# Rows of the paged cache gathered by four tokens and transposed on VectorE in 32x32 blocks, in place of TensorE transposes

## The chip, the cores and the metric

One core of one Trainium2 chip. The metric is the device time of one execution in microseconds. A core has TensorE (PE, with its weight loads PEld), VectorE (DVE), ScalarE (ACT), GpSimd (POOL) and SyncE (SP); each runs its own queue of instructions in order and waits for others by semaphores. SyncE and GpSimd also issue the transfers (DMA) spoken of here.

## What is computed

One step of a decoder layer: a norm, one wide input projection, sparse attention with three branches, a gated MLP branch, an output projection and a final norm, for 512 prompt tokens and for 8 sequences of 4 new tokens with 1,024 cached tokens each. All is in fp32. The change touches only the compression of keys and values, cut here to what matters:

```
CMP_BLOCK, CMP_STRIDE, CMP_HIDDEN, PAGE_SIZE = 32, 16, 128, 128
def compress(rows, params):                       # rows: (B, T, 2 heads, 64)
    w1, b1, w2, b2 = params                       # w1: (32 * 64, 128), w2: (128, 64)
    n_cmp = (T - CMP_BLOCK) // CMP_STRIDE + 1
    idx = arange(n_cmp)[:, None] * CMP_STRIDE + arange(CMP_BLOCK)[None, :]
    blocks = rows[:, idx].transpose(0, 1, 3, 2, 4).reshape(B, n_cmp, G, CMP_BLOCK * dh)
    return gelu(blocks @ w1 + b1) @ w2 + b2
kc = compress(concatenate([pool_k[page_table], k_cmp]), cmp_k)   # sequences: 63 blocks each
vc = compress(concatenate([pool_v[page_table], v_cmp]), cmp_v)
kc, vc of the prompt: compress(k_cmp), compress(v_cmp)           # 31 blocks
```

Each block is 32 tokens by 64 channels of one head, multiplied by w1, a sum over 2,048 values. On the chip it is 16 matmuls that each sum over 128 partitions, so the cached rows, which lie in memory as token by channel, have to be turned so that channels lie on partitions.

## The kernel before

A function `plan()` writes one list of steps, `ORDER`. Every engine walks the same list and does its part of each step, so the list sets the order within each queue, and semaphores set the rest. The steps `main` are groups of 24 fp32r matmuls of the big projections (each fp32 operand is split in a high and a low part, and three products are summed; L1735). The rest of the work is placed between them.

The compression has ten chunks. Chunk 0 is the prompt's keys, 1 to 4 two sequences each for the keys, 5 the prompt's values, 6 to 9 two sequences each for the values (`PAIRS` are the eight cached chunks). The steps of a cached chunk `c`:

- GpSimd (`load`, L912) gathers 128 rows of 8 tokens, 4 KB each, of one sequence into one of three slots of `ring` by an indirect DMA, 512 KB in all; two gathers a chunk. It waits until TensorE has transposed what the slot held.
- `xt` n (n = 0 to 3): TensorE transposes half a slot by four 128x128 transposes (L1881) into one of two PSUM banks `t`, which other steps use too. ScalarE casts it to fp32r as the high part `xt_hi` in two instructions of 64 partitions (L1152). VectorE subtracts to get the low part `xt_lo`, again in halves of 64 partitions (L1456), and does one of ScalarE's casts (L1449). In the list, `xt` 2 and 3 cut the main group of the chunk into three parts (`part`).
- `hidh`: 32 matmuls, w1's high and low parts by `xt_hi` (L1917, L1918). `hidl`: 16 matmuls, w1's high part by `xt_lo` (L1920); it is placed behind the first transposes of the next chunk. ScalarE applies the gelu.
- `kc`: small matmuls with w2 (L1933, L1938), and VectorE adds the bias and for keys the rotation.

A prompt chunk has one `xt` with eight small transposes (L1885), four copies on VectorE (L1439), and one set of 16 plain fp32 matmuls `hid` (L1896).

Also in the stage: `low` and `split` of the next weights (VectorE L1301, ScalarE L1034), which release the next weight loads on SyncE; the layer norm steps `ln`, `ln2` (VectorE); the spatial gate `sp` (TensorE L1871, VectorE L1383 to L1393); `w1hi` and `w1lo`, the split of w1 for keys and later for values. SyncE ties 16 small copies of the query blocks to the step (`xt`, 2, 0) and window-cache copies to `xt` of chunks 1, 3, 6 and 8. GpSimd ties its gathers and, at (`xt`, 9, 0), the first key loads to these steps. `hidh` and `kc` wait also for gelu results, and `xt` of a chunk may overwrite `xt_hi` after `hidh` of the chunk before and `xt_lo` after its `hidl`.

## Time and profile before

| | us |
|---|---|
| three runs, median | 566.74 (565.77 to 567.42) |
| profiled execution, span from first to last instruction | 562.9 |
| the compression stage in it | about 98 to 225 |

The profiled execution has no time of its own on record beside its span; the median lies 3.8 us above the span. In the profile PE and PEld are TensorE's matmuls and weight loads, DVE is VectorE, ACT ScalarE, POOL GpSimd and SP SyncE. L1735 is line 1735 of the kernel before. `t` are the two PSUM banks of the transposes, `so` the PSUM banks of the compression and the scores, `m` those of the main groups, `U` one large SBUF area that holds, among others, the ring. TensorE overlaps successive matmuls, so the distance from one start to the next is what one of them holds, and it is less than its listed duration. "Idle before" is the time that an engine had nothing to do just before an instruction, with what ended it.

### The profile page before, as it was taken

The page shows a single profiled execution, that of the slowest core. Times are in us where ns is not written, and L with a number is a line of the kernel's source. Part 1 is how long each engine was busy: PE and PEld are TensorE (multiplying, and loading weights), DVE is VectorE, ACT ScalarE, POOL GpSimd, SP SyncE. Part 2 cuts the span into 40 slices and gives each one's busy share as a digit, 9 for nine tenths or more (in the row PEclk, how much of TensorE's full clock was granted, in tenths as well). Part 3 has the DMA queues.
Part 4 walks back from the last instruction along what each step waited for, and adds up shares of the span by engine and source line. Part 5 has one row for each costly group of instructions (what it writes and reads, how often), then busy time and mean ns, then how long its engine had stood idle before and what let it go on. Part 6 is the DMA issues. An engine that isn't in the chain of part 4 may idle for free.

```text
span 562.9 us, 12929 instructions
## 1 busy us (share of the span) xinstructions
PE 540.9 (96%) x5214; PEld 490.3 (87%) x5214; DVE 344.9 (61%) x854; ACT 257.2 (46%) x585; POOL 135.0 (24%) x237
## 2 busy tenths in 40 slices
PE   6899999999999999999999999999999999999995
PEld 4899999999988899898897877767788999999995
DVE  5633231398797778567465488686864367773466
ACT  5533424554713443324133378677775352223343
POOL 0016423121201141372400035656336000000000
PEclk9999999999999999999999999999999999999999
DMA  8537822537335452586831155656445624305104
GB/s 296 194 98 230 266 76 77 187 113 216 104 112 208 134 169 76 167 283 243 273 104 40 38 138 149 178 129 157 117 114 133 172 76 146 126 30 186 42 4 158
DMA packets 60239, 81.06 MB, mean 144 GB/s; under 512 B 7506, under 2 KB 48914, under 8 KB 59923
## 3 DMA queue, kind: packets, MB, share of 16 engines
q1 hardware_dynamic: 49088, 49.97, 29.1%
q0 software_dynamic: 10368, 29.14, 16.8%
q10 hardware_dynamic: 722, 1.12, 0.5%
q8 instruction: 42, 0.69, 0.5%
q14 instruction: 19, 0.15, 0.1%
HBM read 65.23 MB, written 8.13 MB: 130 GB/s over the span
## 4 chain that ended last, share of the span: by engine, by line
PE 67%; DVE 7%; issue 1%; ACT 1%; DVEq 0%; ACTq 0%
PE m L1735 44%; PE so L2043 4%; PE so L2050 3%; PE so L1917 2%; PE so L1918 2%; PE so L1920 2%; PE t L1881 2%; PE so L1956 1%; PE so L2004 1%; DVE w_lo L1301 1%; DVE xt_sb L1456 1%; PE m L1819 1%; PE so L2030 1%; PE t L2023 1%; PE t L1979 1%
## 5 line engine op out<-in xcount | busy, mean ns | idle before, releaser
L1735 PE MATMUL m<-h_hi,w_hi 128*128 128x272 f32 x448 | 133.9, 299 | 0.8 <-DVE za L1414 0.5
L1735 PE MATMUL m<-h_hi,w_lo 128*128 128x272 f32 x448 | 129.2, 288 | 0.0
L1735 PE MATMUL m<-h_lo,w_hi 128*128 128x272 f32 x448 | 128.8, 287 | 0.0
L1735 PE MATMUL m<-w_hi,h_hi 128*128 128x256 f32 (+2 forms) x360 | 104.3, 290 | 2.4 <-issue 1.9
L1735 PE MATMUL m<-w_hi,h_lo 128*128 128x256 f32 (+2 forms) x360 | 101.8, 283 | 0.0
L1735 PE MATMUL m<-w_lo,h_hi 128*128 128x256 f32 (+2 forms) x360 | 101.8, 283 | 0.0
L1301 DVE TENSOR_TENSOR w_lo<-raw,w_hi 128x1024 fp32r<-128x1024 f32 (+2 forms) x62 | 71.0, 1154 | 42.9 <-ACT w_hi L1034 42.8
L1735 PEld LDWEIGHTS m<-h_hi,w_hi 128*128 128x128 f32 x448 | 84.3, 188 | 12.2 <-issue 9.6
L1735 PEld LDWEIGHTS m<-h_lo,w_hi 128*128 128x128 f32 x448 | 84.5, 189 | 0.0
L1735 PEld LDWEIGHTS m<-h_hi,w_lo 128*128 128x128 f32 x448 | 84.4, 188 | 0.0
L990 POOL DMA_DIRECT2D U<-p_turn x108 | 58.3, 548 | 102.4 <-DVE p_turn L1641 101.3
L1735 PEld LDWEIGHTS m<-w_hi,h_hi 128*128 128x128 f32 (+1 forms) x360 | 67.7, 188 | 3.9 <-issue 2.1
L1735 PEld LDWEIGHTS m<-w_lo,h_hi 128*128 128x128 f32 (+1 forms) x360 | 68.0, 189 | 0.1
L1735 PEld LDWEIGHTS m<-w_hi,h_lo 128*128 128x128 f32 (+1 forms) x360 | 67.7, 188 | 0.1
L1034 ACT CAST w_hi<-raw 128x1024 fp32r<-128x1024 f32 (+2 forms) x62 | 60.9, 989 | 0.6 <-DMA raw<-in_w_in 0.5
L1456 DVE TENSOR_TENSOR xt_sb<-t,xt_sb 64x512 fp32r<-64x512 f32 x64 | 44.1, 689 | 9.9 <-PE so L1920 5.2
L1152 ACT CAST xt_sb<-t 64x512 fp32r<-64x512 f32 x56 | 32.5, 580 | 37.7 <-PE t L1881 36.4
L1617 DVE CUSTOM_DVE_ANT_0 U<-so,cst 128x512 f32<-128x512 f32 (+3 forms) x64 | 28.7, 484 | 20.1 <-PE so L2043 20.0
L1209 ACT ACTIVATE U<-U,st 128x512 f32<-128x512 f32 (+3 forms) x64 | 30.7, 551 | 18.3 <-DVE st L1630 18.3
L1735 PE MATMUL m<-x_hi,w_lo 128*128 128x272 f32 x128 | 36.8, 288 | 0.0
L1735 PE MATMUL m<-x_hi,w_hi 128*128 128x272 f32 x128 | 36.8, 287 | 0.0
L1735 PE MATMUL m<-x_lo,w_hi 128*128 128x272 f32 x128 | 36.8, 287 | 0.0
(306 smaller groups left out, 935.3 us busy)
## 6 DMA issues: line engine op xcount, KB each, us to landing
raw<-in_w_in SPq DMA_DIRECT2D x36, 512.0 KB, 4.5
U<-in_x_p SPq DMA_DIRECT2D x8, 512.0 KB, 5.5
raw<-in_w_o SPq DMA_DIRECT2D x8, 512.0 KB, 3.5
U<-p_turn POOLq DMA_DIRECT2D x54, 64.0 KB, 2.6
U<-p_turn SPq DMA_DIRECT2D x42, 64.0 KB, 2.9
raw<-in_w_in SPq DMA_DIRECT2D x8, 256.0 KB, 3.9
raw<-in_w_pa SPq DMA_DIRECT2D x8, 256.0 KB, 4.0
...
```

The costliest lines, as they stand in the source:

```text
L990: pool.dma_start(*block_move(s[1], n)).then_inc(p_moved_pool[s[1] % 4], 16)
L1034: ins = nc.scalar.copy(hi, x)
L1152: ins = nc.scalar.copy(turned(xt_hi, r, g, b), TB[t % 2][64 * g:64 * g + 64, :].rearrange("p (q o n) -> p q o n", q=4, o=2))
L1209: ins = nc.scalar.activation(pb[u][:, j, 0:n], pb[u][:, j, 0:n], ACT.Copy, scale=st[:, m + 12 + j:m + 13 + j])
L1301: ins = v.tensor_tensor(lo, x, hi.bitcast(F32), ALU.subtract)
L1456: ins = v.tensor_tensor(turned(xt_lo, r, g, b), TB[(t + m - n) % 2][64 * g:64 * g + 64, :].rearrange("p (q o n) -> p q o n", q=4, o=2), tu ...
L1617: v.tensor_tensor_reduce(pb[u][:, a, 0:n], S[k % 3][:, 0:n], cs("causal")[:, 512 - n:512], 1.0, -3e38, ALU.add, ALU.max, st[:, m + a:m + a ...
L1735: ins = mm(out, lhs(a, k), rhs(b, k), start=(k == 0 and a + b == 0), stop=(k == n - 1 and a == 1))
L1881: ins = pe.transpose(tb[:, q * P:(q + 1) * P], x[:, (2 * q + r) * P:(2 * q + r + 1) * P], ident)
L1917: mm(out[:, 0:256], w, xt_hi[:, x], start=(j == 0), stop=False, skip_group_check=True)
L2043: mm(S[k % 3][:, 0:n], qT[r, 2 * jh + jj, tok(i)], kT[r, y, 0:n], start=True, stop=True).then_inc(p_scored, 1)
L2050: ins = mm(O[64 * g:64 * g + 64, 256 * jh:256 * jh + 256].rearrange("p (j a r) -> p j a r", j=2, a=4), v_tok[:, y, k, g * DH:(g + 1) * DH] ...
```

## The change

The cached rows are gathered by 4 tokens (2 KB) rather than 8, with 128 rows or 256 KB to a gather, four to a chunk; a ring slot holds one such piece and half of the old ring's space becomes three buffers `xt_f`. VectorE turns a whole piece with one transpose of 128x512 in 32x32 blocks from the slot into `xt_f`; partition 32 a + i then holds channel i of a block for the tokens of quarter a, and the rows of w1 are permuted in memory to agree (`quarters`), which also makes its load one 8 KB run per partition. New steps `xh` (ScalarE casts a piece, 128 partitions at a time) and `xl` (VectorE subtracts it) take the place of the halves. The prompt chunks do the same with one piece each, which `hid` reads directly from `xt_f`. The main group is no longer cut by transposes. The transposes `xt` are put in the list one chunk ahead for three pieces and within the chunk for the fourth. The slot is freed by VectorE's transpose (`x_turned`) and `xt_f` by `xl` (`xt_lo_done`) or `hid`.

```diff
-CMP_ROW = 2 * (np.arange(P) % 64) + np.arange(P) // 64
+CMP_GROUP = np.arange(P) % 32
...
     put("group_mod", (p % 16)[:, None])
-    put("cmp_mod", (CMP_ROW % 16)[:, None])
+    put("cmp_mod", (CMP_GROUP % 8 * 4 + p // 32)[:, None])
     return c
...
              7: [("sp", 4), ("mix", u0[0]), ("mix", u0[1])], 8: [("mix", u1[0]), ("mix", u1[1])], 9: [("mix", u1[2])]}
-    order += [("w1hi", 0), ("xt", 0, 0)]
+    turns = iter([("xt", c, n) for c in range(NCH) for n in range(4 if c in PAIRS else 1)])
+    def turn(count):
+        order.extend(itertools.islice(turns, count))
+    order += [("w1hi", 0)]
+    turn(3)
     main(3)
     order += [("hid", 0), ("w1lo", 0)]
+    turn(1)
     for c in range(1, NCH):
...
         if c == 5:
-            order += [("xt", 5, 0)] + behind + [("sp", 0), ("w1hi", 1), ("ln2", 1), ("w1lo", 1), ("ln2", 2), ("ln2", 3), ("hid", 5),
-                                                ("kc", 4), ("sp", 1)]
+            order += behind + [("sp", 0), ("w1hi", 1), ("ln2", 1), ("w1lo", 1), ("ln2", 2), ("ln2", 3), ("hid", 5), ("kc", 4), ("sp", 1)]
+            turn(1)
             main(1)
             continue
-        order += [("xt", c, 0), ("xt", c, 1)] + behind
+        order += [("xh", c, n) for n in range(3)] + behind + [("xl", c, 0)]
+        turn(1)
+        order += [("xh", c, 3)]
         if c == 1:
...
         s, after = take()
-        order += [("part", s, 0, 5), ("xt", c, 2), ("part", s, 5, 7), ("xt", c, 3), ("part", s, 7, 8), ("kc", c - 1), ("hidh", c)]
+        order += [("part", s, 0, KD)] + [("xl", c, n) for n in range(1, 4)] + [("kc", c - 1), ("hidh", c)]
+        turn(3)
         order += ([s] if c != 7 else []) + [x for x in after if x not in (("ln", NT), ("lnr",))] + extra.get(c, [])
...
 RING = 3
-LOADS = [(w, b) for w in ("kc", "vc") for b in ["p"] + list(range(NB))]
-LOAD_AT = {x: n for n, x in enumerate(LOADS)}
+TURNS = [s for s in ORDER if s[0] == "xt"]
+TURN_AT = {s[1:]: n for n, s in enumerate(TURNS)}
 NKEY = 3 * QB
...
-def load_of(c, n):
-    return LOAD_AT[("kc" if c < 5 else "vc", "p" if c % 5 == 0 else 2 * (c % 5 - 1) + n // 2)]
-def load_turned(n):
-    w, b = LOADS[n]
-    c = 0 if w == "kc" else 5
-    return T_AT[("xt", c, 0) if b == "p" else ("xt", c + 1 + b // 2, 2 * (b % 2) + 1)] + 1
 def ring_count(n):
-    return sum(32 if LOADS[k][1] == "p" else 16 for k in range(n % RING, n + 1, RING))
+    return sum(16 if TURNS[k][1] in PAIRS else 64 for k in range(n % RING, n + 1, RING))
...
-        ring = U[:, 8200:11272].rearrange("p (r c) -> p r c", r=RING)
+        ring = U[:, 8200:9736].rearrange("p (r c) -> p r c", r=RING)
+        xt_f = U[:, 9736:11272].rearrange("p (r c) -> p r c", r=RING)
         w1_at = [U[:, 11272:13320].rearrange("p (j n) -> p j n", j=16), za[:, :, :].rearrange("p j t -> p (j t)")[:, 0:2048].rearrange("p (j n) -> p j n", j=16)]
...
         xt_hi, xt_lo = xt_sb[:, 0:2050], xt_sb[:, 2050:4100]
-        xtp = [x[:, 0:512].rearrange("p (q g m) -> p q g m", q=4, g=G) for x in (sg_flat, U)]
         hid_at = [U[:, 13320:13576], U[:, 13576:13832]]
...
-        def turned(x, r, g, b):
-            return x[64 * r:64 * r + 64, 0:2048].rearrange("p (q o g b n) -> p q o g b n", q=4, o=2, g=G, b=2)[:, :, :, g, b, :]
+        def turned(x, c, n):
+            b, half = divmod(n, 2)
+            return x[:, 0:2048].rearrange("p (k b m i) -> p k b m i", b=2, m=2, i=32)[:, :, b, half, :]
+        def in_blocks(c, n):
+            return xt_f[:, TURN_AT[c, n] % RING, :].rearrange("p (k i) -> p k i", i=32)
...
                 elif s[0] == "load_w1":
-                    sp.dma_start(w1_at[0], w1k.rearrange("(j p) n -> p j n", p=P)).then_inc(w1_loaded[0], 16)
-                    sp.dma_start(w1_at[1], w1v.rearrange("(j p) n -> p j n", p=P)).then_inc(w1_loaded[1], 16)
+                    sp.dma_start(w1_at[0], w1k).then_inc(w1_loaded[0], 16)
+                    sp.dma_start(w1_at[1], w1v).then_inc(w1_loaded[1], 16)
                 elif s[0] == "xt" and s[2] == 0 and s[1] % 5 in (1, 3):
...
-            def load(n):
-                w, b = LOADS[n]
-                if n >= RING:
-                    pool.wait_ge(t_done, load_turned(n - RING))
-                dst, done = ring[:, n % RING, :], ring_loaded[n % RING]
-                if b == "p":
+            def load(t):
+                _, c, n = TURNS[t]
+                if t >= RING:
+                    pool.wait_ge(x_turned, t - RING + 1)
+                dst, done = ring[:, t % RING, :], ring_loaded[t % RING]
+                if c not in PAIRS:
                     pool.wait_ge(cmp_out, 32)
-                    src = (pk_cmp if w == "kc" else pv_cmp).rearrange("(m o r) c -> o m (r c)", o=2, r=8)
-                    for o in range(2):
+                    src = (pv_cmp if c else pk_cmp).rearrange("(m o r) c -> o m (r c)", o=4, r=4)
+                    for o in range(4):
                         pool.dma_start(dst[32 * o:32 * o + 32, :], src[o, :, :]).then_inc(done, 16)
                 else:
-                    src = {"kc": ck_cmp, "vc": cv_cmp}[w]
-                    pool.indirect_dma_start(dst, None, src, bass.IndirectOffsetOnAxis(cmp_rows[:, b:b + 1], 0)).then_inc(done, 16)
+                    b = 2 * (c % 5 - 1) + n // 2
+                    src = ck_cmp if c < 5 else cv_cmp
+                    pool.indirect_dma_start(dst, None, src, bass.IndirectOffsetOnAxis(cmp_rows[:, n % 2, b:b + 1], 0)).then_inc(done, 16)
...
                     pool.dma_start(s_chunk, vg[0:TS, NT, :]).then_inc(out_done, 16)
-                elif s[0] == "xt" and s[2] % 2 == 0:
-                    load_upto(load_of(s[1], s[2]) + RING + 1)
+                elif s[0] == "xt":
+                    load_upto(TURN_AT[s[1:]] + RING + 1)
                     if s[1:] == (NCH - 1, 0):
...
                     ins.then_inc(w1_hi_done, 1)
-                elif kind == "xt" and s[1] in PAIRS:
-                    c, n = s[1], s[2]
-                    b, r = divmod(n, 2)
-                    act.wait_ge(t_done, t + 1)
+                elif kind == "xh":
+                    _, c, n = s
+                    act.wait_ge(x_turned, TURN_AT[c, n] + 1)
                     if c > 1:
                         act.wait_ge(hid_half, PAIRS.index(c))
-                    if c == 6:
-                        act.wait_ge(hid_sum, 6)
-                    for g in range(G - n // 3):
-                        ins = nc.scalar.copy(turned(xt_hi, r, g, b), TB[t % 2][64 * g:64 * g + 64, :].rearrange("p (q o n) -> p q o n", q=4, o=2))
-                    ins.then_inc(xt_hi_done, 1)
+                    nc.scalar.copy(turned(xt_hi, c, n), in_blocks(c, n)).then_inc(xt_hi_done, 1)
                 elif kind in ("hid", "hidl"):
...
                 elif kind == "xt":
-                    c, n = s[1], s[2]
-                    b, r = divmod(n, 2)
-                    tb = TB[t % 2]
-                    dve.wait_ge(t_done, t + 1)
-                    if c % 5 == 0:
-                        if c:
-                            dve.wait_ge(hid_half, 4)
-                        for r in range(2):
-                            for g in range(G):
-                                ins = v.tensor_copy(xtp[c // 5][64 * r:64 * r + 64, :, g, :],
-                                                    tb[64 * g:64 * g + 64, 256 * r:256 * r + 256].rearrange("p (q m) -> p q m", q=4))
-                        ins.then_inc(t_dve, 1)
-                        continue
-                    if n == 2:
-                        continue
+                    k = TURN_AT[s[1:]]
+                    dve.wait_ge(ring_loaded[k % RING], ring_count(k))
+                    if k >= RING:
+                        c = TURNS[k - RING][1]
+                        if c in PAIRS:
+                            dve.wait_ge(xt_lo_done, 4 * PAIRS.index(c) + TURNS[k - RING][2] + 1)
+                        else:
+                            dve.wait_ge(hid_sum, c + 1)
+                    v.transpose(xt_f[:, k % RING, :], ring[:, k % RING, :]).then_inc(x_turned, 1)
+                elif kind == "xl":
+                    _, c, n = s
+                    dve.wait_ge(xt_hi_done, 4 * PAIRS.index(c) + n + 1)
                     if c > 1:
                         dve.wait_ge(hid_sum, c - (c == 6))
-                    at = PAIRS.index(c)
-                    if n == 3:
-                        v.tensor_copy(turned(xt_hi, 1, 1, 1), tb[64:128, :].rearrange("p (q o n) -> p q o n", q=4, o=2)).then_inc(xt_hi_dve, 1)
-                    for m in range(2 if n == 3 else n, n + 1):
-                        b, r = divmod(m, 2)
-                        dve.wait_ge(xt_hi_done, 4 * at + m + 1)
-                        for g in range(G):
-                            if m == 3 and g == 1:
-                                dve.wait_ge(xt_hi_dve, at + 1)
-                            ins = v.tensor_tensor(turned(xt_lo, r, g, b), TB[(t + m - n) % 2][64 * g:64 * g + 64, :].rearrange("p (q o n) -> p q o n", q=4, o=2),
-                                                  turned(xt_hi, r, g, b).bitcast(F32), ALU.subtract)
-                        ins.then_inc(t_dve, 1)
+                    v.tensor_tensor(turned(xt_lo, c, n), in_blocks(c, n), turned(xt_hi, c, n).bitcast(F32), ALU.subtract).then_inc(xt_lo_done, 1)
                 elif kind == "kc":
...
                     ins.then_inc(t_done, 1)
-                elif kind == "xt":
-                    c, n = s[1], s[2]
-                    ld = load_of(c, n)
-                    pe.wait_ge(ring_loaded[ld % RING], ring_count(ld))
-                    x = ring[:, ld % RING, :]
-                    if c % 5:
-                        r = n % 2
-                        for q in range(4):
-                            ins = pe.transpose(tb[:, q * P:(q + 1) * P], x[:, (2 * q + r) * P:(2 * q + r + 1) * P], ident)
-                    else:
-                        for k in range(8):
-                            r, q = divmod(k, 4)
-                            ins = pe.transpose(tb[:, k * 64:k * 64 + 64], x[0:64, (2 * q + r) * P:(2 * q + r + 1) * P], ident[0:64, 0:64])
-                    ins.then_inc(t_done, 1)
                 elif kind == "hid":
                     c = s[1]
+                    k = TURN_AT[c, 0]
                     pe.wait_ge(w1_loaded[c // 5], 16)
-                    wait_evacuated(pe, T_AT[("xt", c, 0)])
+                    pe.wait_ge(x_turned, k + 1)
                     if c >= 2:
                         pe.wait_ge(hid_ready, c - 1)
+                    x = xt_f[:, k % RING, :].rearrange("p (r g e m) -> p r e g m", r=4, g=G, e=2)
                     for j in range(16):
-                        o = j // 4
-                        at = 32 * (o % 2) + o // 2
-                        ins = mm(S[c % 2][:, 0:2 * NCP], w1_at[c // 5][:, j, :], xtp[c // 5][:, j % 4, :, at:at + NCP], start=(j == 0), stop=(j == 15))
+                        o, r, e = j // 8, j // 2 % 4, j % 2
+                        ins = mm(S[c % 2][:, 0:2 * NCP], w1_at[c // 5][:, j, :], x[:, r, e, :, o:o + NCP], start=(j == 0), stop=(j == 15))
                     ins.then_inc(hid_sum, 1)
...
                         pe.wait_ge(xt_hi_done, 4 * PAIRS.index(c) + 4)
-                        pe.wait_ge(xt_hi_dve, PAIRS.index(c) + 1)
                         if c >= 2:
...
                     else:
-                        for n in range(4):
-                            wait_evacuated(pe, T_AT[("xt", c, n)])
+                        pe.wait_ge(xt_lo_done, 4 * PAIRS.index(c) + 4)
                     for j in range(16):
-                        o, q = divmod(j, 4)
-                        x = slice(512 * q + 256 * (o % 2) + o // 2, 512 * q + 256 * (o % 2) + 256 + o // 2)
+                        o, r, e = j // 8, j // 2 % 4, j % 2
+                        def x(part):
+                            return part[:, 512 * r + o:512 * r + o + 512].rearrange("p (g e n) -> p e g n", g=G, e=2)[:, e, :, :]
                         w = w1_hi[j // 8][:, j % 8, :]
                         if first:
-                            mm(out[:, 0:256], w, xt_hi[:, x], start=(j == 0), stop=False, skip_group_check=True)
-                            ins = mm(out[:, 0:256], w1_lo[:, j, :], xt_hi[:, x], start=False, stop=False, skip_group_check=True)
+                            mm(out[:, 0:256], w, x(xt_hi), start=(j == 0), stop=False, skip_group_check=True)
+                            ins = mm(out[:, 0:256], w1_lo[:, j, :], x(xt_hi), start=False, stop=False, skip_group_check=True)
                         else:
-                            ins = mm(out[:, 0:256], w, xt_lo[:, x], start=False, stop=(j == 15), skip_group_check=True)
+                            ins = mm(out[:, 0:256], w, x(xt_lo), start=False, stop=(j == 15), skip_group_check=True)
                     ins.then_inc(hid_half if first else hid_sum, 1)
...
+    def quarters(a):
+        return A(a).reshape(2, 4, 8, 32, P).transpose(1, 3, 0, 2, 4).reshape(P, 16, P)
     def column(a):
...
         ("x_p", A(x_prompt).reshape(TP, D)), ("x_s", A(x_sample).reshape(TS, D)),
-        ("ck_cmp", A(cache_k_cmp).reshape(-1, 8 * P)), ("cv_cmp", A(cache_v_cmp).reshape(-1, 8 * P)),
+        ("ck_cmp", A(cache_k_cmp).reshape(-1, 4 * P)), ("cv_cmp", A(cache_v_cmp).reshape(-1, 4 * P)),
         ("ck_sel", A(cache_k_sel).reshape(-1, 8 * P)), ("cv_sel", A(cache_v_sel).reshape(-1, 8 * P)),
         ("ck_win", A(cache_k_win).reshape(NB, 512, P)), ("cv_win", A(cache_v_win).reshape(NB, 512, P)),
-        ("pages", np.concatenate([A(page_table).T[np.arange(P) // 16], A(page_table).T[CMP_ROW // 16]], 1)),
-        ("w_in", A(w_in)[0]), ("w1k", A(cmp_k_w1)[0]), ("w1v", A(cmp_v_w1)[0]), ("w_sp", A(w_spatial)[0].transpose(1, 0, 2)),
+        ("pages", np.concatenate([A(page_table).T[np.arange(P) // 16], *(A(page_table).T[4 * m + CMP_GROUP // 8] for m in range(2))], 1)),
+        ("w_in", A(w_in)[0]), ("w1k", quarters(cmp_k_w1)), ("w1v", quarters(cmp_v_w1)), ("w_sp", A(w_spatial)[0].transpose(1, 0, 2)),
         ("w_pa", A(w_pa)[0]), ("w_pb", A(w_pb)[0]), ("w_o", A(w_o)[0]), ("norm_g", A(norm_g).reshape(1, D)), ("final_g", rows(final_g)),
...
```

## Rows read from the trace of the kernel before

**Rows 1.** The page of the kernel before: span and busy time of each engine.
```profile
span 562.9 us, 12929 instructions
...
PE 540.9 (96%) x5214; PEld 490.3 (87%) x5214; DVE 344.9 (61%) x854; ACT 257.2 (46%) x585; POOL 135.0 (24%) x237
```

**Rows 2.** Windows: stretch, its us, busy us (instructions) of PE, PEld, DVE, ACT, POOL, clock, DMA share, GB/s.
```profile
98.00:225.00 127.00, 121.79 (x1079) 116.00 (x1079) 95.07 (x184) 56.09 (x100) 23.82 (x26) 1.00 0.45 146
130.00:142.00 12.00, 11.90 (x104) 11.28 (x105) 9.91 (x21) 5.43 (x11) 2.24 (x3) 1.00 0.65 208
154.00:178.40 24.40, 21.86 (x181) 20.25 (x181) 22.69 (x43) 8.32 (x14) 2.79 (x4) 1.00 0.36 112
```

**Rows 3.** Chain that ended last, one chunk: start us, us, engine, tile, line, count.
```profile
130.91 0.36 PE so L1917
...
134.94 0.88 PE t L1881 x8
...
135.81 1.90 PE so L1920 x16
...
139.59 0.44 PE t L1881 x4
...
142.38 0.36 PE so L1917
```

**Rows 4.** Groups by form, 98 to 225 us: the work the change removes.
```profile
L1881 PE MATMUL t<-cst,U 128*128 128x128 f32 x128 | 19.1, 278 | 2.1 <-DVE sg L1393 2.0
...
L1456 DVE TENSOR_TENSOR xt_sb<-t,xt_sb 64x512 fp32r<-64x512 f32 x64 | 44.1, 689 | 9.9 <-PE so L1920 5.2 <-ACT xt_sb L1152 3.5
...
L1449 DVE CAST xt_sb<-t 64x512 fp32r<-64x512 f32 x8 | 5.6, 695 | 5.7 <-PE t L1881 5.6
...
L1152 ACT CAST xt_sb<-t 64x512 fp32r<-64x512 f32 x56 | 32.5, 580 | 37.7 <-PE t L1881 36.4
```

**Rows 5.** Timeline of PE: transposes of a prompt chunk.
```profile
157.84 0.71 PE L1885 MATMUL t<-cst,U 64*128 64x64 f32 x8
```

**Rows 6.** Groups by form, whole span: nearest rows for what it adds.
```profile
L1494 DVE STREAM_TRANSPOSE U<-U 128x512 f32<-128x512 f32 x19 | 11.9, 673 | 0.0
...
L1301 DVE TENSOR_TENSOR w_lo<-raw,w_hi 128x512 fp32r<-128x512 f32 x8 | 5.1, 678 | 0.0
...
L1034 ACT CAST w_hi<-raw 128x512 fp32r<-128x512 f32 x8 | 4.5, 616 | 0.0
```

**Rows 7.** Chain that ended last: matmuls whose moving operand comes in short runs.
```profile
345.50 1.88 PE so L2050 x16
```

**Rows 8.** DMA issues, 98 to 225 us and then 177 to 183 us: count, median us to landing.
```profile
U<-in_cv_cmp,cmp_rows POOLq DMA_INDIRECT x8, 4.7
...
U<-in_ck_sel,half_rows POOLq DMA_INDIRECT x4, 3.9
...
U<-in_cv_cmp,cmp_rows POOLq DMA_INDIRECT x1, 9.0
```

**Rows 9.** Timelines of DVE and POOL: descriptor writing beside VectorE work.
```profile
124.38 1.21 DVE L1301 TENSOR_TENSOR w_lo<-raw,w_hi 128x1024 fp32r<-128x1024 f32 x1
...
124.63 1.78 POOL L912 DMA_INDIRECT U<-in_ck_cmp,cmp_rows  x1 [5.24 <-PE t L1881]
...
221.87 3.07 DVE L1494 STREAM_TRANSPOSE U<-U 128x512 f32<-128x512 f32 x5
...
223.57 0.95 POOL L931 DMA_INDIRECT turned_late<-in_ck_sel,half_rows  x1 [15.46 <-PE so L1920]
```

**Rows 10.** Timeline of PE: first hi product of chunks 1, 4, 6 and 9.
```profile
119.45 0.35 PE L1917 MATMUL so<-xt_sb,w_hi 128*128 128x256 f32 x1 [0.92 <-DVE xt_sb L1449]
...
153.88 0.36 PE L1917 MATMUL so<-xt_sb,w_hi 128*128 128x256 f32 x1
...
178.39 0.36 PE L1917 MATMUL so<-xt_sb,w_hi 128*128 128x256 f32 x1 [0.36 <-DVE xt_sb L1449]
...
217.35 0.35 PE L1917 MATMUL so<-xt_sb,w_hi 128*128 128x256 f32 x1
```

18 lines of the change are left out of this document (10 added, 8 removed).

## The prediction

> **What bounds the kernel now.** I read the page first, then the busy time by stretch, then the chain of waits through the compression, then the groups of the instructions that the diff touches. The page shows TensorE busy for 540.9 of 562.9 us and no other engine near it [rows 1]. The compression runs from about 98 to 225 us. There TensorE is busy 121.8 of 127.0 us at the full granted clock (1.00, the 2.4 GHz level), VectorE 95.1, ScalarE 56.1 and GpSimd 23.8 [rows 2]. So at most 5.2 us of idle TensorE can be won there; the rest must come from instructions taken off TensorE. Two kinds of stretch differ. In an ordinary chunk (130 to 142 us) TensorE is busy 11.90 of 12.0 us and VectorE 9.91: TensorE sets the pace. In the change from keys to values (154 to 178.4 us) VectorE is busy 22.69 of 24.4 us and TensorE 21.86: there VectorE sets it, with the layer norm, the split of the second w1 and the spatial gate in one queue [rows 2]. The chain of waits through an ordinary chunk is TensorE end to end, from one `hidh` (L1917) at 130.91 to the next at 142.38, 11.47 us. Its transposes stand in that chain as 8 in 0.88 us and twice 4 in 0.44, so 0.11 us for each [rows 3].
>
> **What the change removes.** TensorE: 16 transposes in each of eight cached chunks, 128 in all [rows 4]. Their mean of 278 ns is latency; they follow one another every 0.11 us, so they hold TensorE for 128 x 0.11 = 14.1 us. The two prompt chunks lose 8 half-size transposes each, 8 in about 0.65 to 0.71 us [rows 5], 1.3 us together. That is 15.4 us off the engine that sets the end. With them go the waits for a free `t` bank: the transposes waited 2.1 us, 2.0 of it behind the spatial gate's additions on VectorE (L1393) [rows 4]. One of these waits lies in the VectorE-bound stretch, so I count 1.0. VectorE loses, per cached chunk, 8 subtractions of 689 ns and one copy of 695 ns, 6.2 us; ScalarE loses 7 casts of 580 ns, 4.1 us [rows 4].
>
> **What it adds.** Per cached chunk VectorE gets four 128x512 block transposes and four 128x512 subtractions with both inputs in SBUF, ScalarE four 128x512 casts out of SBUF. All three have near relatives in the trace: the transposes of the keys take 673 ns, the 128x512 weight subtraction 678, the 128x512 weight cast 616 [rows 6]. VectorE: 4 x (0.673 + 0.678) = 5.4 us against 6.2, so 0.8 less; ScalarE 2.5 against 4.1. The old instructions used 64 partitions at a time and the new ones 128, which is why an added job does not add time. Only the prompt chunks and the transition change more: four copies per prompt give way to one transpose. The bounds for these prices are narrow (the strided 32-element runs of the output might cost up to the 695 ns of the slowest row, 0.1 us per chunk).
>
> The matmuls keep their number. Their moving operand changes from one run of 256 columns to two of 128. Matmuls of 256 columns in runs of 32 pace at 1.88/16 = 0.118 us [rows 7], the same as the old `hidl` at 1.90/16 [rows 3]; I take nothing. If each of the 384 matmuls lost 10 ns, it would be 3.8 us; that upper end is my estimate from the resolution of these rows.
>
> GpSimd gets 32 gathers of 256 KB for 16 of 512 KB. It has 100 us of idle time in the stage, and one issue takes about 1 us. What matters is the latency: the old gathers landed in 4.7 us (median), a 256 KB gather of the keys, also in 2 KB rows, in 3.9, and one old gather that met the window-cache copies in 9.0 [rows 8]. The ring still has three slots, but each holds half a batch, so half as much is prefetched, and the slot is freed on VectorE. The third transpose for a chunk uses a slot freed by the fourth of the chunk before. Behind it VectorE has three subtractions, the `kc` step (perhaps 1 of the 3.7 us that its 9.9 holds beside the 6.2 of `xt`) and two transposes, 2.0 + 1.0 + 1.3 = 4.3 us, about the landing time plus the wake-up. The fourth uses the slot freed by the first: until it is wanted TensorE runs `hidh` and `hidl`, 4.0 + 1.9 = 5.9 us [rows 3], so it lands in time unless delayed. Then subtraction, transpose and cast (2.0 us) lie beside the main group and `kc`, 3.8 us (11.5 - 4.0 - 1.9 - 1.8 of transposes): 1.8 us of slack, less what VectorE is late. An undisturbed gather costs nothing, one of 6 us makes VectorE wait but hardly TensorE. Behind a waiting transpose stand the weight split, layer norm and the next subtractions on VectorE, and TensorE's `hidh` waits for them. The 9.0 us gather comes again, where eight window copies go out together near chunk 7: 4.3 us late less the slack and work it covers, about 2 us. I take 2.3 us over the whole stage (0 if nothing is late, about 9 if every chunk loses 1.1).
>
> A contention is to be weighed here. One gather's descriptor writing took 1.78 us, begun while a VectorE subtraction from two SBUF inputs ran, where one beside five block transposes took 0.95 [rows 9]. Taken as a cost, 0.8 us on some gathers fits into the 2.3. The Trainium skill ("SBUF — State Buffer", section "Who interferes with whom") says that `tensor_tensor` with two SBUF inputs takes only the shared read interface, and infers that descriptor writing is not held up; by it this part is zero, by the row up to 0.8 us for a gather, and the trace's single long one speaks mildly against the inference.
>
> The moved steps also carry SyncE work. The 16 copies of the query blocks (`xt` 2,0) and the window copies (`xt` 1, 3, 6, 8) now stand ahead of the weight loads which the same chunk's `low` releases. These weight tiles are split only chunks later, so they cost nothing; without this cover a raw load would be late by the issue time of the 16 copies. The w1 loads become 8 KB runs; they are done long before 98 us, no gain. Key loads on GpSimd follow the last gathers as before.
>
> **The sum.** Chunk 1 waited 0.92 us for its `xt` copies [rows 10]; with the transpose of its fourth piece done about 1 us before TensorE arrives, that goes. Between chunks 4 and 6 (153.88 to 178.39, 24.5 us) VectorE rules, so I followed its queue: it loses 8 subtractions, a copy and 4 prompt copies, about 7.9 us, and gains 5 transposes and about 2 subtractions, 4.7; 3.2 less, of which 0.8 goes back to a wait for the first spatial-gate product. That leaves 2.4, just what TensorE loses there (16 x 0.11 + 0.65), so the stretch keeps its full share and TensorE waits there about as long as now. From chunk 6 to 9 (178.39 to 217.35) three more chunks and 1.0 of bank waits. Total: 15.4 + 0.9 + 1.0 = 17.3, less 2.3 for late gathers, 15.0. After 225 us nothing is changed and TensorE is the bound, so an earlier start is kept. The profiled execution spans 562.9 us, which becomes 547.9. The runs' median, 566.74, lies 3.8 above the span (that execution has no time of its own beside it), and I keep the 3.8: 551.7 us.
>
> **Rivals.**
> Late gathers. The half-size ring makes VectorE wait about 1 to 1.5 us per chunk and the layer norm and splits push it onto TensorE. For it: half the prefetch, the 9.0 us row, two transposes per chunk with no margin. Against: 1.8 us of slack. It gives back a further 4 to 9 us: 556 to 561. Chance 0.18.
> VectorE becomes the bound. In a chunk with layer norm and split it has about 8.7 us (9.9 busy in 12 us scaled to 11.5, less 0.8) of TensorE's 9.7 (11.47 less 1.76). A price 0.15 us higher for each of the eight instructions brings it to 9.9, and with the waits for `hidl` near 10.5: 0.8 us lost on eight chunks, 6.4: 558. Chance 0.07. The Trainium skill ("VectorE: DVE Perf Modes", section "Rules for kernel authors") speaks against the move: a 128x128 transpose belongs on TensorE if PSUM will do, VectorE being the fastest only for 32x32 blocks. The trace agrees on price (0.44 us for four blocks on TensorE, 0.673 on VectorE), but not on what is scarce here.
> Slower. One mechanism: the three-slot ring becomes a round trip. Four pieces per chunk through three slots need 4/3 x (landing + 0.8) us; that passes the old 11.5 us when gathers land in 7.8 us or more. At 9.0 for all, a chunk takes 13.1 us, 1.6 more on six or seven chunks, less the 3 us won outside them: about 574 us. Against: only one gather in the stage took so long. Chance 0.05.
> The change does not pay, because the transposes are hidden anyway: the chain of waits has them in it, so only if VectorE governs every chunk; 565 to 567. Chance 0.03.
> The forecast's own case, 548 to 555: 0.67.
>
> The range reaches from 547.0 (no late gather, most of the remaining idle gone: 566.74 - 19.7) to 560.0, which leaves 0.05 to 0.1 above with the last two rivals and little below. A difference under 0.3% (1.7 us) could not be told from none. Faster 0.91, same 0.03, slower 0.06.
>
> **What would show it.** Right: no PE rows for L1881 and L1885; `hidh` to `hidh` near 9.7 us in chunks 2 to 4; VectorE's transposes near 0.67, subtractions near 0.68, casts near 0.62; TensorE idle for 2 to 3 us ahead of chunk 6 and in chunk 7; 225 us becoming about 210. Wrong: `hidh` matmuls above 0.12 us apiece, transposes ended by a DMA in most chunks, gathers landing in 6 us, or the 15 us won at 225 us given back before the first `qkS`.

## The result, and the profile after

The changed kernel takes 551.43 us (median of 4 runs, 550.79 to 552.57) where the kernel before takes 566.73 (565.77 to 567.42) on the same chip. The ratio on record is 0.9745, 95% interval 0.9724 to 0.9767; the two medians alone give 0.9730, inside it. The profiled execution took 550.91 us itself, with a span of 549.2. That is 13.7 us less span than before, where the medians differ by 15.3.

The page: span, and busy time of each engine (for [rows 1]).

```profile
span 549.2 us, 12605 instructions
...
PE 526.3 (96%) x5070; PEld 478.4 (87%) x5070; DVE 332.7 (61%) x840; ACT 242.0 (44%) x561; POOL 156.4 (28%) x257
```

Windows, columns as in [rows 2]: first the whole stage, then three places that matter below.

```profile
98.00:225.00 127.00, 120.59 (x1148) 115.78 (x1152) 91.59 (x185) 46.60 (x86) 49.23 (x49) 0.99 0.52 168
130.00:140.00 10.00, 8.80 (x76) 8.44 (x75) 7.23 (x19) 5.28 (x8) 3.44 (x4) 1.00 0.98 357
165.00:170.00 5.00, 2.62 (x23) 2.31 (x21) 4.86 (x9) 2.19 (x5) 2.26 (x2) 0.96 0.24 56
170.00:180.00 10.00, 9.96 (x72) 9.99 (x73) 6.40 (x14) 2.22 (x5) 3.37 (x4) 0.85 0.73 262
```

Timeline of TensorE: the first hi product of each cached chunk, 1, 2, 3, 4, 6, 7, 8, 9 (for [rows 10]; in brackets TensorE's idle time before it).

```profile
116.55 0.38 PE L1893 MATMUL so<-xt_sb,w_hi 128*128 128x256 f32 x1
...
126.74 0.36 PE L1893 MATMUL so<-xt_sb,w_hi 128*128 128x256 f32 x1 [0.71 <-ACT xt_sb L1151]
...
137.55 0.36 PE L1893 MATMUL so<-xt_sb,w_hi 128*128 128x256 f32 x1 [1.20 <-ACT xt_sb L1151]
...
147.79 0.36 PE L1893 MATMUL so<-xt_sb,w_hi 128*128 128x256 f32 x1
...
170.04 0.55 PE L1893 MATMUL so<-xt_sb,w_hi 128*128 128x256 f32 x1 [2.41 <-ACT xt_sb L1151]
...
182.76 0.38 PE L1893 MATMUL so<-xt_sb,w_hi 128*128 128x256 f32 x1
...
193.56 0.39 PE L1893 MATMUL so<-xt_sb,w_hi 128*128 128x256 f32 x1
...
203.15 0.38 PE L1893 MATMUL so<-xt_sb,w_hi 128*128 128x256 f32 x1
```

From start to start, with the kernel before beside it (a start is read at the same place in both traces; "possible" is the shortest that any later run showed):

| chunk to chunk | before | after | saved | possible |
|---|---|---|---|---|
| start of 1 | 119.45 | 116.55 | 2.90 | - |
| 1 to 2 | 11.46 | 10.19 | 1.27 | 9.66 |
| 2 to 3 | 11.47 | 10.81 | 0.66 | 9.53 |
| 3 to 4 | 11.50 | 10.24 | 1.26 | 9.56 |
| 4 to 6 | 24.51 | 22.25 | 2.26 | 19.50 |
| 6 to 7 | 14.48 | 12.72 | 1.76 | 11.34 |
| 7 to 8 | 13.03 | 10.80 | 2.23 | 10.74 |
| 8 to 9 | 11.45 | 9.59 | 1.86 | 9.58 |

14.20 us are won by chunk 9 and 13.7 are left at the end. Two things stand in the table: an undisturbed chunk takes 9.6 us (8 to 9 here), and none of the first three distances does so.

Groups of instructions by form, 98 to 225 us: what was added (for [rows 4, 6]).

```profile
L1437 DVE STREAM_TRANSPOSE U<-U 128x512 f32<-128x512 f32 x34 | 22.7, 693 | 7.7 <-DMA U<-in_cv_cmp,cmp_rows 3.5 <-DMA U<-in_ck_cmp,cmp_rows 3.4
L1443 DVE TENSOR_TENSOR xt_sb<-U,xt_sb 128x512 fp32r<-128x512 f32 x32 | 20.4, 677 | 3.8 <-PE so L1896 2.2 <-ACT xt_sb L1151 1.4
L1151 ACT CAST xt_sb<-U 128x512 fp32r<-128x512 f32 x32 | 18.6, 617 | 35.6 <-DVE U L1437 19.0 <-PE so L1894 16.7
L1893 PE MATMUL so<-xt_sb,w_hi 128*128 128x256 f32 x128 | 33.2, 297 | 4.4 <-ACT xt_sb L1151 4.3
```

The prices are near those of the prediction (0.693, 0.677, 0.617 us). VectorE's transposes waited 6.9 us for gathers. The place that TensorE felt is this, in the timelines of GpSimd, SyncE and VectorE:

```profile
129.47 0.94 POOL L915 DMA_INDIRECT U<-in_ck_cmp,cmp_rows  x1 [2.24 <-DVE U L1437]
```

```profile
130.03 0.54 SPq L826 DMA_DIRECT2D out_sk_win<-in_ck_win  x1
...
134.51 0.59 SPq L827 DMA_DIRECT2D out_sv_win<-in_cv_win  x1
```

```profile
135.93 0.71 DVE L1437 STREAM_TRANSPOSE U<-U 128x512 f32<-128x512 f32 x1 [2.37 <-DMA U<-in_ck_cmp,cmp_rows]
...
141.61 0.71 DVE L1437 STREAM_TRANSPOSE U<-U 128x512 f32<-128x512 f32 x1 [1.00 <-DMA U<-in_ck_cmp,cmp_rows]
```

Eight window copies are issued within 4.5 us right behind the gather, the DMA share goes to 0.98 (window 130 to 140), and the transpose of chunk 3's last piece starts 6.46 us after the gather's issue. In the kernel before, SyncE issued them so (first and last of each group):

```profile
137.30 0.59 SPq L824 DMA_DIRECT2D out_sk_win<-in_ck_win  x1
...
139.20 0.59 SPq L825 DMA_DIRECT2D out_sv_win<-in_cv_win  x1
...
174.87 0.52 SPq L824 DMA_DIRECT2D out_sk_win<-in_ck_win  x1
...
179.55 0.59 SPq L825 DMA_DIRECT2D out_sv_win<-in_cv_win  x1
```

Chunk 3's four copies left alone, and chunk 6's four left together with chunk 8's. Now chunk 6's four leave together with chunk 3's, at 130 us, and chunk 8's alone, at 168.70 to 170.87. In ScalarE's timeline one sees how this lateness reaches the start of chunk 4 (L1134 is the square root, L1163 the gelu):

```profile
143.47 0.21 ACT L1134 ACTIVATE st<-st 128x5 f32<-128x5 f32 x1 [3.64 <-DVE st L1359]
143.59 1.65 ACT L1151 CAST xt_sb<-U 128x512 fp32r<-128x512 f32 x3
145.25 1.28 ACT L1163 ACT_TABLE_LOAD   x1
146.55 0.47 ACT L1163 ACTIVATE U<-so,prm 128x256 f32<-128x256 f32 x1
```

The layer norm's statistics stand behind the waiting transpose on VectorE; ScalarE's square root waits for them, behind it stand chunk 4's casts, a change of function table and the gelu, and for this gelu TensorE's `kc` products waited 0.51 us.

### The profile page after: what moved, and what is told of

It reads as the page before. It is cut to its first block, busy times and chain, and to the rows that moved or that the text cites. A ratio compares the mean times of both kernels' runs of the same rounds, so it can differ in the third digit from the quotient of the medians.

```text
span 549.2 us, 12605 instructions
## 1 busy us (share of the span) xinstructions
PE 526.3 (96%) x5070; PEld 478.4 (87%) x5070; DVE 332.7 (61%) x840; ACT 242.0 (44%) x561; POOL 156.4 (28%) x257
## 4 chain that ended last, share of the span: by engine, by line
PE 77%; DVE 12%; issue 4%; DMA 3%; ACT 3%; DVEq 0%; ACTq 0%
PE m L1722 54%; PE so L2019 5%; PE so L2026 3%; DMA U<-in_ck_cmp,cmp_rows 2%; PE m L1806 2%; DVE U L1437 2%; PE so L1893 2%; DVE w_lo L1300 2%; PE so L1894 2%; PE so L1896 1%; PE so L1932 1%; DVE xt_sb L1443 1%; PE so L1980 1%; PE t L1748 1%; PE so L2006 1%
## 5 line engine op out<-in xcount | busy, mean ns | idle before, releaser
L1207 ACT ACTIVATE U<-U,st 128x512 f32<-128x512 f32 (+3 forms) x64 | 30.8, 551 | 18.4 <-DVE st L1617 18.4
L1893 PE MATMUL so<-xt_sb,w_hi 128*128 128x256 f32 x128 | 33.2, 297 | 4.4 <-ACT xt_sb L1151 4.3
L1198 ACT ACTIVATE U<-U,st 128x512 f32<-128x512 f32 (+3 forms) x64 | 35.1, 551 | 3.3 <-DVE st L1608 3.3
```

Of the source, the lines that this page charges most:

```text
L1198: ins = nc.scalar.activation(pb[u][:, j, 0:n], pb[u][:, j, 0:n], ACT.Exp, bias=st[:, m + 4 + j:m + 5 + j], scale=SCALE, accum_out=st[:, m ...
L1207: ins = nc.scalar.activation(pb[u][:, j, 0:n], pb[u][:, j, 0:n], ACT.Copy, scale=st[:, m + 12 + j:m + 13 + j])
L1893: mm(out[:, 0:256], w, x(xt_hi), start=(j == 0), stop=False, skip_group_check=True)
```

## The experiments

Each kernel is the changed one with one more edit. In the diffs `...` marks what is left out. Spans are set against its 549.2 (549.1 in the repeat), ratios are to the kernel before on the same chip in the same hour: 565.09 us in the first group (e1 to e4), 568.81 in the second (e5 to e8), 565.14 in the third (e9 to e12). Spans of the second group are not set against 549.2, since its chip is slower. By the intervals of the ratios e11 and e12 are faster than the change and e1, e5, e6 and e7 slower; e2, e3, e4, e8 and e10 are not clear of it, and what is said of them rests on their traces, of one execution each.

**e1: the transposes back on TensorE alone.** Sixteen per cached chunk, of a constant into an unused bank; nothing reads them.

```diff
+                elif kind == "xt" and s[1] in PAIRS:
+                    for q in range(4):
+                        pe.transpose(O[:, q * P:(q + 1) * P], ident, ident)
```

> The changed kernel, with the 128 transposes of the cached chunks put back on TensorE, four at each xt step, turning the identity matrix into an unused PSUM bank that nobody reads; no engine waits for them, VectorE's transposes and everything else stay. Theory (the gain is the time that the transposes held TensorE): they add 14.1 us of work, of which the idle that TensorE has in the changed kernel (0.7, 1.2, 0.5 us ahead of chunks 2, 3, 4, 2.4 ahead of chunk 6, and 1.7 lost to the low clock) swallows up to 6, so 8 to 12 us slower than the changed kernel, about 559 to 563 us. Rival (the gain came from the waits around the transposes: evacuation from PSUM, the shared t banks, the cut main groups): under 4 us slower, 555 us or less.

558.15 us, ratio 0.9881 [0.9849, 0.9913]; span 556.4, 7.2 more. The first hi product of chunks 2 and 3:

```profile
128.88 0.38 PE L1896 MATMUL so<-xt_sb,w_hi 128*128 128x256 f32 x1
...
140.25 0.39 PE L1896 MATMUL so<-xt_sb,w_hi 128*128 128x256 f32 x1
```

Chunks 3, 4, 7, 8 and 9 take 11.37, 11.34, 13.10, 12.58 and 11.37 us, each 1.74 to 1.82 above e12, the kernel with the fewest other disturbances: 0.11 us per transpose, as predicted. The 11.34 to 11.37 us of chunks 3, 4 and 9 lie only 0.1 us under the 11.45 to 11.50 of the kernel before, so what an ordinary chunk won is nearly all the transposes' time, and little is left for the waits around them. Chunk 4 to 6 takes 21.99, no more than without them: there TensorE waited anyway (1.53 us of idle time instead of 2.41). The total, 7.2 us, lies under the 8 to 12 expected and far above the rival's 4. The changed kernel had waits in which the load hides, and its clock fell once behind the wait of 2.41 us, which it does not do here; against e12, which has neither, the load costs 556.4 - 545.4 = 11.0 us.

**e2: no late gathers.** The cached gathers are left out after the first three ring slots, so this kernel works on old rows.

```diff
-    return sum(16 if TURNS[k][1] in PAIRS else 64 for k in range(n % RING, n + 1, RING))
+    return sum((16 if k < RING else 0) if TURNS[k][1] in PAIRS else 64 for k in range(n % RING, n + 1, RING))
...
+                if t >= RING and c in PAIRS:
+                    return
```

> The changed kernel without its cached gathers after the first two pieces (all others are left out, so the compression works on old data; the two prompt loads stay). Theory (late gathers cost what the chunks 2 to 4 took above 9.7 us and a little): the waits of VectorE for a DMA vanish, chunk 3 starts 1.2 us sooner, chunk 4 about 0.5; in all 1.5 to 2.5 us faster than the changed kernel, 549 to 550 us; the 0.7 us ahead of chunk 2, where no transpose waited for a DMA, and the 2.4 us ahead of chunk 6 stay. Rival (the ring of half-size slots holds the whole stage back): 4 us or more faster, and the waits ahead of chunks 2 and 6 shrink too.

547.89 us, 0.9699 [0.9665, 0.9734]; span 546.2, 3.0 less where 1.5 to 2.5 were expected. Chunks 3 and 4 come to 9.53 and 9.56. Chunk 2 still starts 0.70 us late and chunk 6 2.41 us late: neither is a gather's doing.

**e3: window copies early**, at four places between 59 and 89 us.

```diff
-                elif s[0] == "xt" and s[2] == 0 and s[1] % 5 in (1, 3):
+                elif s in (("gates",), ("rope", 2), ("gr",), ("rope", 3)):
```

> The changed kernel with the 16 window-cache copies issued by SyncE at four steps between about 60 and 95 us, before the compression, and not at the xt steps. Theory (the gathers are late only where eight window copies go out together, at 130 to 135 us and again at 169 us): the 2.4 us wait of the transpose in chunk 3 and the one in chunk 7 go, 1 to 2 us faster than the changed kernel, 549.5 to 550.5. Rival (gathers of 2 KB rows are slow by themselves): the landings stay near 5 to 6 us, no difference from the changed kernel.

548.12 us, 0.9696 [0.9662, 0.9730]; span 546.3, 2.9 less, and chunks 3 and 4 at 9.55 and 9.56: the same as without gathers. Of the 2.9 us 1.9 are won in these two chunks (2.4 against e9) and 0.3 in 4 to 6; 0.8 lie ahead of chunk 1, whose start differs as much between e3 (115.78) and e12 (116.53), which are alike up to there. So in chunks 3 and 4 the gathers are late only beside the copies. One expectation failed: ahead of chunk 7 VectorE's transpose still waits 2.02 us for its gather (171.34), with no copy near it, though TensorE does not feel it. Undisturbed gathers land in 4.0 and 3.5 us, the DMA issues of this run between 98 and 225 us say (count, us to landing):

```profile
U<-in_cv_cmp,cmp_rows POOLq DMA_INDIRECT x16, 3.5
...
U<-in_ck_cmp,cmp_rows POOLq DMA_INDIRECT x14, 4.0
```

**e4: chunk 6 turned early.** Its last transpose, casts and first subtraction go right behind `hid` of chunk 5, ahead of two layer-norm steps.

```diff
-            order += behind + [("sp", 0), ("w1hi", 1), ("ln2", 1), ("w1lo", 1), ("ln2", 2), ("ln2", 3), ("hid", 5), ("kc", 4), ("sp", 1)]
+            order += behind + [("sp", 0), ("w1hi", 1), ("ln2", 1), ("w1lo", 1), ("hid", 5)]
             turn(1)
+            order += [("xh", 6, n) for n in range(3)] + [("xl", 6, 0)]
+            turn(1)
+            order += [("xh", 6, 3), ("ln2", 2), ("ln2", 3), ("kc", 4), ("sp", 1)]
             main(1)
...
+        if c != 6:
...
```

> The changed kernel with only the order of VectorE's and ScalarE's queues changed between chunks 5 and 6: the last two transposes of chunk 6, its casts and its first subtraction stand right behind hid of chunk 5, ahead of the layer norm of tiles 2 and 3, kc 4 and sp 1. 
549.05 us, 0.9710 [0.9684, 0.9737]; span 546.9. Chunk 4 to 6 falls to 19.75 us, with no idle time ahead of chunk 6, and its products take 3.98 us, at full clock, where they took 5.30 in the changed kernel. But chunk 4 started 11.56 us after chunk 3, since its `kc` waited 1.8 us for the gelu; e9 shows that this wait is not of the edit. And TensorE now waits 0.56 us ahead of chunk 7. The full clock is of this execution: its mean is 0.997, and two of the other three show 0.994.

**e5: the wait ahead of chunk 6 filled** with 20 products that nothing reads.

```diff
+                        if c == 6:
+                            for _ in range(20):
+                                mm(O[:, 0:256], ident, cst[:, 0:256], start=True, stop=True)
```

> The changed kernel with 20 matmuls of 256 columns (identity by constants, into an unused PSUM bank that nobody reads) ahead of the first hi product of chunk 6, where TensorE otherwise waits 2.4 us for ScalarE's cast of the fourth piece. Theory (the granted clock falls to 1.2 GHz for 3.4 us because TensorE had stood idle): hidh of chunk 6 starts at the same distance from that of chunk 4 (about 22.2 us), the clock stays at its upper level, its length is 3.9 instead of 5.3 us, and the kernel is 1.3 to 1.8 us faster than the changed one, about 549.9 us. Rival (the fall has nothing to do with the wait): the fall stays, no difference.

558.87 us, 0.9823 [0.9806, 0.9839]. The filling was over three times as long as the wait, as the timeline of TensorE shows:

```profile
170.60 8.90 PE L1879 MATMUL so<-cst 128*128 128x256 f32 x40
```

Chunk 6's products took 4.02 us at full clock, which is what was asked, but chunk 4's took 5.41, behind an idle time of 1.7 us. As a price this run says nothing; e10 does it again.

**e6: the next chunk's turn ahead of the layer norm**, to free chunk 2's start from VectorE's queue.

```diff
-        order += [("xh", c, 3)]
+        order += [("xh", c, 3)] + held
+        held = []
...
+        if c < 4:
+            held, after = after + extra.get(c, []), []
...
```

> The changed kernel with, for chunks 1 to 3, the layer norm and weight split that follow a chunk moved in the list behind the fourth transpose of the next chunk. Theory (the 0.7 us wait ahead of chunk 2 is VectorE's queue, which had layer norm and weight split between the third and the fourth transpose): the wait ahead of chunk 2 goes, the one ahead of chunk 3 shrinks only by what is not the late gather; 0.7 to 1.5 us faster than the changed kernel. Rival (it is the latency of the gather that follows the transposes): no difference, or the wait shows up as one for a DMA.

557.99 us, 0.9822 [0.9802, 0.9841]: slower than the change, where 0.7 to 1.5 us less were expected. The profiled execution is the fastest of the four (554.64). In it the wait ahead of chunk 2 shrinks (0.70 to 0.17 us, 9.66 us for the chunk), so it was this queue. But the rival came too: at 136.54 VectorE's transpose waits 3.88 us for its gather, this falls fully on chunk 3 as 2.7 us of idle time, and then the clock is at half, the windows say. The chunk's products took 6.56 us.

```profile
136.00:138.00 2.00, 0.00 (x0) 0.00 (x0) 1.42 (x3) 0.71 (x2) 0.48 (x1) 0.83 0.90 347
138.00:140.00 2.00, 1.84 (x8) 1.87 (x9) 1.83 (x8) 0.20 (x1) 0.47 (x1) 0.50 0.97 381
140.00:142.00 2.00, 2.00 (x11) 2.00 (x11) 1.97 (x5) 0.00 (x0) 0.00 (x0) 0.50 0.34 129
```

**e7: every gather one turn later**, so that in effect the ring has two slots.

```diff
-                    pool.wait_ge(x_turned, t - RING + 1)
+                    pool.wait_ge(x_turned, t - RING + 2)
```

> The changed kernel with each gather issued one transpose later (it waits for the transpose two before its own, not three, as with a ring of two slots). Theory (the gather's landing of 4 to 5 us is covered by 4.3 to 5.9 us of work and little more): the third and the fourth piece of a chunk now are 3 to 4 us late each and VectorE, by then with only 1 us to spare, hands 2 to 3 us a chunk to TensorE: 14 to 24 us slower than the changed kernel, 566 to 576 us. Rival (there is slack enough for another such delay): under 5 us.

569.75 us, 1.0016 [1.0000, 1.0032]. One slot less costs (1.0016 - 0.9745) x 568.8 = 15.4 us: all that the change had won. Chunks 2 and 3 take 13.49 and 15.86 us, with 2.9 and 3.0 us of idle time ahead of them, and the first spatial-gate product waits 4.2 us. Not all of it is the gathers' lateness as such: the clock was at half for 24 us of the stage (3.4 in the change), 13.7 of them behind the last of these waits.

```profile
170.00:175.00 5.00, 5.00 (x24) 5.00 (x24) 2.87 (x6) 0.00 (x0) 0.00 (x0) 0.50 0.21 65
```

**e8: e3, e4 and e6 together.**

> The changed kernel with three edits together: window copies early, the last transposes of chunk 6 early, layer norm and weight split behind the fourth transpose in chunks 1 to 3. Theory (the three waits are separate): 2.8 + 2.3 + 0.7 = 5.8 us faster than the changed kernel by the runs so far and the 0.7 expected; 544 to 547 us, span near 543.5, and chunk to chunk 9.6 us in 1 to 4. Rival (one hides another): 2 us less than the sum, 547 us or more.

555.51 us, 0.9734 [0.9668, 0.9800], with single runs from 548.78 to 556.37: the 5.8 us of the theory did not come. In the profiled one TensorE stood still for 2.7 us ahead of the first spatial-gate product and then ran at half clock for 13 us:

```profile
152.50:155.00 2.50, 0.00 (x0) 0.00 (x0) 2.24 (x6) 2.31 (x3) 1.54 (x2) 0.85 0.73 220
155.00:165.00 10.00, 9.94 (x49) 9.53 (x50) 5.45 (x8) 0.80 (x3) 0.09 (x1) 0.50 0.19 65
```

Chunks 2 to 4 take 9.90, 10.40 and 10.14 us, and in each of them VectorE's transpose waits for its gather (1.40, 1.94 and 1.70 us) although the window copies are gone. e11, the same without the edit of e6, takes 10.19, 9.53 and 9.56 us and waits 0.8 us ahead of the spatial gate. So it is the order of e6 that spoils the sum; what makes the spatial gate wait longer with it was not followed.

**e9: the change again, unaltered**, as a base for the last three.

> The changed kernel, with nothing altered, timed again beside the three others so that they can be set against it on one chip. Both theories expect the ratio of the first measurement, 0.9745 (0.972 to 0.977), and a profile in which chunk 3 starts 10.8 us after chunk 2, chunk 6 starts 22.2 us after chunk 4 behind 2.4 us of idle time, and chunk 7 12.7 us later with a granted clock of 0.5 at the start of chunk 6.

551.12 us, 0.9748 [0.9725, 0.9771]; span 549.1. Chunk 3 starts after 10.02 us and chunk 4 after 11.53, where it was 10.81 and 10.24: together 2.4 us over e12's, where it was 1.9, and here mostly at `kc`.

```profile
147.13 0.66 PE L1909 MATMUL so<-U,prm 128*64 128x126 f32 x8 [1.78 <-ACT U L1163]
```

**e10: the wait filled with 5 products.** The edit of e5 with `range(5)`.

> The filled wait again with 5 products in place of 20, since one of them took 0.43 us in the earlier run (8.6 us for 20), so that they take about 2.2 us, the length of the idle time ahead of chunk 6. Theory that the clock falls because TensorE has stood still: the clock is full in chunk 6's first products, these take 3.9 us rather than 5.3, chunk 7 then starts 11.4 to 12.6 us after chunk 6 (it may wait for its own turned data instead), and the span is 0 to 1.4 us shorter than the changed kernel's. Rival, that the clock falls there for another reason (the transfers at 370 to 416 GB/s in those microseconds, or the time since the last fall): it falls to 0.5 although TensorE never stands still, and the products take over 5 us.

549.70 us, 0.9733 [0.9709, 0.9758]; span 548.0. The window 170 to 175 us, first of e9 and then of e10:

```profile
170.00:175.00 5.00, 4.92 (x29) 4.95 (x30) 2.35 (x5) 0.12 (x1) 2.46 (x3) 0.66 1.03 379
```

```profile
170.00:175.00 5.00, 5.00 (x44) 5.00 (x44) 2.72 (x7) 1.04 (x2) 2.15 (x3) 1.00 1.02 381
```

The DMA load is the same and the clock is full: here the fall came with standing still, not with the transfers. Chunk 6's products take 3.93 us rather than 5.39 and 4 to 7 takes 33.41 rather than 35.01 us, 1.6 less. The span wins only 1.1, since in this execution chunk 4 met the fall instead (2.3 us of idle time for the gelu, then 5.08 us for its products).

**e11: e3 and e4 together**, without e6.

> The two cheapest repairs together: the window copies issued before chunk 1, and chunk 6's last transposes and casts right behind chunk 5's hidden products. If their savings are of different waits they add up: chunk 3 after 9.6 us rather than 10.8 (1.2), and chunks 6 and 7 as in the run with chunk 6 early (2.3 to 2.9 less the longer wait of chunk 4's keys), so a span of 545 to 546.5 and a ratio near 0.967. Rival, that with chunk 3 early the waiting time appears again ahead of chunk 4's keys and in chunk 6, so that the sum is no better than one of them: a span of 546.3 to 547 and a ratio of 0.970.

544.68 us (5 runs, 543.99 to 545.60), 0.9628 [0.9605, 0.9651]; span 543.9, 5.2 less than e9 and 1.1 under the range expected. This is the fastest kernel of the study, 20.5 us under the one before. Chunks 3 and 4 take 9.54 and 9.56, 4 to 6 19.50, 6 to 7 11.41. The savings do more than add up, since two waits of e4, 1.8 us for the gelu and 0.56 us ahead of chunk 7, are gone too; the first at least was the copies' doing. What is left of waits of TensorE between 98 and 225 us:

```profile
PE t L1862 <- DVE U L1372: 0.8, 1, 0.8
PE so L1897 <- ACT xt_sb L1155: 0.7, 1, 0.7
PE t L1779 <- ACT qT L1135: 0.4, 2, 0.2
```

**e12: e3 and e10 together.**

> The window copies issued before chunk 1, and 5 filling products ahead of chunk 6. With full clock in chunk 6 and chunk 3 early: a span of 545 to 546.3, that is 0 to 1.3 us less than with the copies alone (546.3). Rival, that chunk 7 waits for its gathered rows instead of running slowly: 546.3 again, with about 1.4 us of idle time of TensorE ahead of chunk 7, released by the last cast of chunk 7's turned data.

546.72 us, 0.9668 [0.9645, 0.9691]; span 545.4, 0.9 less than with the copies alone. Chunk 6's products take 3.94 us (5.45 in e3) and 6 to 7 takes 11.36 (12.88 in e3), with no wait ahead of chunk 7. The window 167 to 172 us, first of e3 and then of e12:

```profile
167.00:172.00 5.00, 4.94 (x28) 4.97 (x29) 2.98 (x6) 0.10 (x1) 2.43 (x3) 0.66 0.69 219
```

```profile
167.00:172.00 5.00, 4.93 (x39) 4.54 (x38) 3.81 (x7) 0.87 (x2) 3.01 (x3) 1.00 0.72 230
```

This is not of the profiled execution alone: the mean granted clock is 0.998 or 0.999 in all five runs of e12, 0.990 to 0.997 in the four of e3 and 0.991 to 0.995 in the nine of the change.

## Why the prediction was right, and where it was not

The case forecast, faster by the transposes' time less some late gathers, is what happened, and 551.43 is 0.3 us from 551.7. Several terms were off and cancel in part, so that a distance of only 0.3 us is luck (item 9).

1. **The transposes, 15.4 us.** Right in price: e1 shows 1.74 to 1.82 us for sixteen wherever TensorE sets the pace. Not all of it was on the path: chunk 4 to 6 took the dummies for nothing.
2. **VectorE's and ScalarE's new work.** Right: 0.693, 0.677, 0.617 us for 0.673, 0.678, 0.616.
3. **Two runs of 128 columns, no cost.** Right to within 0.1 us a chunk. From the first start to the last the 16 lo products take 1.83 us in six chunks and 1.91 and 1.93 in chunks 6 and 7 (1.82 to 1.87 before), the 32 of a hi half at full clock 3.79 to 3.85 (3.74 to 3.77 before): about 0.6 us in all where nothing was counted.
4. **The gross gain, 17.3 us** (transposes, chunk 1's wait, bank waits, before anything is late). Right: in e12, with the gathers on time and the clock full, the span is 562.9 - 545.4 = 17.5 us shorter. That kernel still has the 0.7 us of item 6 ahead of chunk 2. An undisturbed chunk takes 9.53 to 9.59 us for the 9.7 foreseen.
5. **Late gathers, 2.3 us.** Right in size: 1.9 us in chunks 3 and 4, 2.4 in the repeat. That is luck in part, for the place was wrong, and with it the term that took the moved SyncE work as free. The working followed which weight loads the copies now stand ahead of, not which copies would leave together: those of chunks 3 and 6 leave at 130.03 to 134.51, beside chunk 3's gathers, and only four are left near chunk 7. Chunk 7's transpose does wait 2.40 us, at 174.71, but TensorE has no idle time ahead of chunk 7: chunk 6's products are slow there (in e4, at full clock, it waits 0.56 us). And part of the cost went a way that the working had not: through the square root and the gelu on ScalarE to `kc` (0.51 us, 1.78 in e9).
6. **VectorE's queue ahead of chunk 2, 0.7 us,** was not counted. VectorE's 8.7 of 9.7 us was an average; the layer norm and the weight split lie between the third and the fourth transpose, and there the order matters, not the sum (e6). The gross gain was met all the same, since other chunks won more (2.23 in 7 to 8). Outside the change from keys to values this is all that the rival "VectorE becomes the bound" came to. With item 5 it is also why the sign "near 9.7 us in chunks 2 to 4" did not show: they took 10.19, 10.81 and 10.24.
7. **Chunk 4 to 6, 2.4 saved and 2 to 3 us of idle time.** Right: 2.26 and 2.41. The step that failed is "TensorE waits there about as long as now": before, TensorE waited 2.5 us in four pieces, 0.36 ahead of chunk 6 [rows 10] and the rest at the spatial gate, `hid` and a `t` bank; now it waits 3.5 us in two, 2.41 of them in one piece, and with it the clock was at half for 3.4 us. The clock cost 1.5 us in chunks 6 and 7 (e12 against e3) and is the term missing from the sum. From e12's 17.5 to the 13.7 measured it is 1.9 in chunks 3 and 4, 0.3 in 4 to 6, 1.4 in 6 to 7 and 0.2 behind the stage. In chunk 7, where TensorE was also foreseen idle, it was not.
8. **The rival with a round trip of the ring** did not come, but e7 shows how near it lay: one slot less and all the gain is gone, the clock's part included.
9. **The 3.8 us between span and median.** Wrong in kind. All thirteen profiled executions with a time of their own took 1.7 to 1.8 us more than their span (550.91 for 549.2 in the changed kernel), so 562.9 was an execution of about 564.7, under the fastest of the recorded runs (565.77). The span's gain is 13.7, not 15.0; the medians' was 15.3 here and 565.14 - 551.12 = 14.0 in e9. That the forecast hit by 0.3 us is these misses cancelling: 1.3 us too much gain, 2.1 too much between span and time (3.8 for 1.7), and a median that lies 0.5 above the profiled execution.

What stays open: why the delay of chunk 3's gathers falls once on `hidh` (1.20 us) and once on `kc` (1.78), and why the kernel before takes 3.7 us more on the chip of the second group (in the traces of e5 to e8 the part behind the last `hidl` takes about 2 us more than in the others, 342.1 to 343.0 us for 339.9 to 340.7). No run was made for either.
